# Gate and up biases of the routed experts: from one-hot matmul products to rows repeated by DMA and added by VectorE

## The reference

```
logits = xf @ router_w + router_b             # 32 experts, top 4 per token
gu  = xb @ w_gu[e] + b_gu[e]                  # xb: 128 tokens of expert e; w_gu[e] is 1024 x 2048
glu = minimum(gu[:, :1024], 7)                # the gate half
lin = clip(gu[:, 1024:], -7, 7)               # the up half
act = glu * sigmoid(1.702 * glu) * (lin + 1)
y   = act @ w_dn[e] + b_dn[e]                 # w_dn[e] is 1024 x 1024
```

## Time and profile before

| | |
|---|---|
| median of 3 runs | 2343.35 us (2341.95 to 2346.4) |
| the profiled execution, its own time | 2342.93 us |
| its span | 2341.1 us |
| mean granted TensorE clock | 0.948 of full |
| the 34 units | from about 825 us to 2308 us of the span |

### The profile page before, as it was taken

One profiled execution on the slowest core, in us unless ns is written; L12 is line 12 of the kernel. 1 busy time (PEld: TensorE's weight loads), 2 busy tenths in 40 slices (PEclk: granted clock), 3 DMA queues, 4 the chain that ended last, 5 costly groups with the idle time before them and its releaser, 6 DMA issues.

```text
span 2341.1 us, 41559 instructions
## 1 busy us (share of the span) xinstructions
PE 2165.4 (92%) x15487; PEld 1731.2 (74%) x15487; DVE 1834.0 (78%) x2152; ACT 1366.4 (58%) x1545; POOL 552.2 (24%) x434
## 2 busy tenths in 40 slices
PE   6899999867899399999999999999999999999994
PEld 5667888755678377778778778778778778778773
DVE  3699999948733777877877877877877877877885
ACT  4542223865742457667667667667667667667665
POOL 1007786764000102112112112112112112112110
PEclk8779999967999699999999999999999999999997
DMA  5011211020023279889889889889889889889896
GB/s 142 19 46 37 55 45 54 24 75 35 1 84 126 96 267 340 310 290 346 309 287 348 309 285 348 312 285 351 310 282 349 310 285 348 312 286 344 315 374 256
DMA packets 253598, 526.46 MB, mean 225 GB/s; under 512 B 33048, under 2 KB 59800, under 8 KB 253180
## 3 DMA queue, kind: packets, MB, share of 16 engines
q1 hardware_dynamic: 240268, 483.27, 57.6%
q0 software_dynamic: 13264, 42.34, 7.5%
HBM read 490.96 MB, written 35.91 MB: 225 GB/s over the span
## 4 chain that ended last, share of the span: by engine, by line
PE 70%; DMA 10%; DVE 8%; ACT 4%; issue 4%; POOL 2%; SPq 0%; DVEq 0%; ACTq 0%; POOLq 0%
PE ps L1754 13%; PE ps L1756 12%; PE ps L1755 12%; DMA e_raw<-in_w_gate_up_dram 9%; PE ps L1761 9%; PE ps L1429 5%; PE ps L1430 5%; PE ps L1431 5%; DVE e_wlo L2253 2%; PE ps L1766 1%; PE ps L1504 1%; PE ps L1634 1%; PE ps L1645 1%; PE ps L1584 1%; DVE a_s L2031 1%
## 5 line engine op out<-in xcount | busy, mean ns | idle before, releaser
L1312 ACT ACTIVATE e_whi<-e_raw 128x2048 fp32r<-128x2048 f32 x411 | 786.2, 1918 | 421.3 <-PE ps L1756 309.0
L2253 DVE TENSOR_TENSOR e_wlo<-e_raw,e_whi 128x2048 fp32r<-128x2048 f32 x410 | 926.8, 2286 | 66.3 <-ACT e_whi L1312 64.8
L1754 PE MATMUL ps<-e_whi,xh 128*128 128x512 f32 x1088 | 434.7, 400 | 0.0
L1755 PE MATMUL ps<-e_whi,xl 128*128 128x512 f32 x1088 | 424.3, 390 | 0.0
L1756 PE MATMUL ps<-e_wlo,xh 128*128 128x512 f32 x1088 | 424.1, 390 | 0.0
L941 POOL DMA_INDIRECT x_d<-ym,scur x34 | 70.6, 2078 | 871.0 <-ACT ym L1345 850.8
L1754 PEld LDWEIGHTS ps<-e_whi,xh 128*128 128x128 f32 x1088 | 204.3, 188 | 52.7 <-issue 12.9
L1756 PEld LDWEIGHTS ps<-e_wlo,xh 128*128 128x128 f32 x1088 | 204.3, 188 | 43.9
L1755 PEld LDWEIGHTS ps<-e_whi,xl 128*128 128x128 f32 x1088 | 204.5, 188 | 39.4
L1754 PE MATMUL ps<-e_whi,ath 128*128 128x512 f32 x544 | 221.7, 408 | 12.9 <-DVE atl L2281 12.9
L1756 PE MATMUL ps<-e_wlo,ath 128*128 128x512 f32 x544 | 213.3, 392 | 0.0
(11 more groups left out here) (351 smaller groups left out, 3345.1 us busy)
## 6 DMA issues: line engine op xcount, KB each, us to landing
e_raw<-in_w_gate_up_dram SPq DMA_DIRECT2D x275, 1024.0 KB, 5.2
e_raw<-in_w_down_dram SPq DMA_DIRECT2D x136, 1024.0 KB, 11.4
w_raw<-in_w_in_dram SPq DMA_DIRECT2D x20, 512.0 KB, 3.8
xt<-in_x_dram SPq DMA_DIRECT2D x8, 512.0 KB, 6.2
xr<-in_x_dram SPq DMA_DIRECT2D x8, 512.0 KB, 4.2
x_d<-x SPq DMA_DIRECT2D x8, 512.0 KB, 2.6
h_d<-h SPq DMA_DIRECT2D x8, 512.0 KB, 2.9
x<-x_d SPq DMA_DIRECT2D x8, 512.0 KB, 7.4
```

Of the source, the lines that this page charges most:

```text
L1312: nc.scalar.activation(e_whi[:, m % HRING, :], e_raw[:, m % RING, :], ACT.Copy).then_inc(s.e_hi, 1)
L1754: nc.tensor.matmul(dst, a_hi, slot_hi, start=False, stop=False, skip_group_check=True)
L1755: nc.tensor.matmul(dst, a_lo, slot_hi, start=False, stop=False, skip_group_check=True)
L2253: nc.vector.tensor_tensor(e_wlo[:, m % HRING, :], e_raw[:, m % RING, :], e_whi[:, m % HRING, :].bitcast(F32), ALU.subtract).then_inc(s.e_l ...
```

## The change

Gate and up biases no longer go through TensorE for the main tokens of a unit. SP loads the two bias rows of the unit's expert, each repeated into all 128 partitions, into `bgate` and `bup` (2 DMAs of 512 KB); VectorE adds them in place of the plain read of PSUM and limits the sum in a second operation, in place. The first product of a tile now starts the accumulation. SP issues the two loads for the next unit between its pieces 1 and 2, after a wait for the first operation of `a_out(1)` of the current unit, which is the last reader of the tiles. For the first unit they stand ahead of the store and the load of lines 733 and 734. The down bias and the biases of the overflow tokens stay as they were.

```diff
+        bgate = at("bgate", F_ + 108 * KB, [P, D])
+        bup = at("bup", F_ + 135 * KB, [P, D])
...
+            def load_biases(e):
+                for k, dst in enumerate((bgate, bup)):
+                    sp.dma_start(dst[:], I["b_gate_up"][0, bass.ds(e, 1), D * k:D * k + D].to_broadcast([P, D])).then_inc(s.ld_bgu, 16)
             def loads(u, here, after, following):
                 for m in range(3, PIECES):
                     load(u, m, here)
-                for m in range(3):
+                for m in range(2):
                     load(Unit(u.loop, u.a, u.b + 1, after), m, following)
+                sp.wait_ge(s.e_act, u.nth(12, 12 + 6 + 3))
+                load_biases(following)
+                load(Unit(u.loop, u.a, u.b + 1, after), 2, following)
...
             sp.wait_ge(s.v_be, BE_STEPS)
+            load_biases(e0)
...
             def sigmoid(u, j):
-                act.wait_ge(s.e_act, u.nth(8, 8 + 4 * j + 1))
+                act.wait_ge(s.e_act, u.nth(12, 12 + 6 * j + 2))
...
                 if half == 0:
-                    pe.wait_ge(s.e_act, u.nth(8, 4 * j + (6 if g else 5)))
-                    bias_into(ps[:, g, :], sel[:], D * g + 512 * j)
+                    pe.wait_ge(s.e_act, u.nth(12, 6 * j + (9 if g else 7)))
...
-                    m = three(ps[:, g, :], xh[:, buf, k, :], xl[:, buf, k, :], hi_[:, c, :], lo_[:, c, :], half == 1 and c == 3)
+                    m = three(ps[:, g, :], xh[:, buf, k, :], xl[:, buf, k, :], hi_[:, c, :], lo_[:, c, :], half == 1 and c == 3,
+                              k == 0)
...
             def g_out(u, j):
                 dve.wait_ge(s.p_pc, u.nth(PIECES, 4 * j + 2 + RING))
-                nc.vector.tensor_scalar(gm[:], ps[:, 0, :], LIMIT, None, ALU.min).then_inc(s.e_act, 1)
+                if j == 0:
+                    dve.wait_ge(s.ld_bgu, u.nth(32, 32))
+                nc.vector.tensor_tensor(gm[:], ps[:, 0, :], bgate[:, 512 * j:512 * j + 512], ALU.add).then_inc(s.e_act, 1)
+                dve.wait_ge(s.e_act, u.nth(12, 12 + 6 * j + 1))
+                nc.vector.tensor_scalar(gm[:], gm[:], LIMIT, None, ALU.min).then_inc(s.e_act, 1)
             def a_out(u, j):
                 dve.wait_ge(s.p_pc, u.nth(PIECES, 4 * j + 4 + RING))
-                nc.vector.tensor_scalar(um[:], ps[:, 1, :], LIMIT, -LIMIT, ALU.min, ALU.max).then_inc(s.e_act, 1)
-                dve.wait_ge(s.e_act, u.nth(8, 8 + 4 * j + 2))
+                nc.vector.tensor_tensor(um[:], ps[:, 1, :], bup[:, 512 * j:512 * j + 512], ALU.add).then_inc(s.e_act, 1)
+                dve.wait_ge(s.e_act, u.nth(12, 12 + 6 * j + 3))
+                nc.vector.tensor_scalar(um[:], um[:], LIMIT, -LIMIT, ALU.min, ALU.max).then_inc(s.e_act, 1)
+                dve.wait_ge(s.e_act, u.nth(12, 12 + 6 * j + 4))
```

More of the change, by code:

```diff
@@ L303, in __init__ @@
         self.ld_bias = sem("ld_bias")
+        self.ld_bgu = sem("ld_bgu")
         self.a_bias = sem("a_bias")
@@ L1750, in xo_transposes, with three @@
                 m.then_inc(s.p_xo, 1)
-            def three(dst, a_hi, a_lo, slot_hi, slot_lo, last):
-                nc.tensor.matmul(dst, a_hi, slot_hi, start=False, stop=False, skip_group_check=True)
+            def three(dst, a_hi, a_lo, slot_hi, slot_lo, last, first=False):
+                nc.tensor.matmul(dst, a_hi, slot_hi, start=first, stop=False, skip_group_check=True)
                 nc.tensor.matmul(dst, a_lo, slot_hi, start=False, stop=False, skip_group_check=True)
@@ L1798, in gu_step @@
                     k = 4 * half + c
-                    m = three(ps[:, g, :], xh[:, buf, k, :], xl[:, buf, k, :], hi_[:, c, :], lo_[:, c, :], half == 1 and c == 3)
+                    m = three(ps[:, g, :], xh[:, buf, k, :], xl[:, buf, k, :], hi_[:, c, :], lo_[:, c, :], half == 1 and c == 3,
+                              k == 0)
                 m.then_inc(s.p_pc, 1)
             def a_transposes(u, v, j):
-                pe.wait_ge(s.e_act, u.nth(8, 8 + 4 * j + 4))
+                pe.wait_ge(s.e_act, u.nth(12, 12 + 6 * j + 6))
                 for q in range(4):
@@ L2265, in g_out @@
                 dve.wait_ge(s.p_pc, u.nth(PIECES, 4 * j + 2 + RING))
-                nc.vector.tensor_scalar(gm[:], ps[:, 0, :], LIMIT, None, ALU.min).then_inc(s.e_act, 1)
+                if j == 0:
[3 more added lines that the diff above has]
+                nc.vector.tensor_scalar(gm[:], gm[:], LIMIT, None, ALU.min).then_inc(s.e_act, 1)
             def a_out(u, j):
                 dve.wait_ge(s.p_pc, u.nth(PIECES, 4 * j + 4 + RING))
-                nc.vector.tensor_scalar(um[:], ps[:, 1, :], LIMIT, -LIMIT, ALU.min, ALU.max).then_inc(s.e_act, 1)
-                dve.wait_ge(s.e_act, u.nth(8, 8 + 4 * j + 2))
+                nc.vector.tensor_tensor(um[:], ps[:, 1, :], bup[:, 512 * j:512 * j + 512], ALU.add).then_inc(s.e_act, 1)
+                dve.wait_ge(s.e_act, u.nth(12, 12 + 6 * j + 3))
+                nc.vector.tensor_scalar(um[:], um[:], LIMIT, -LIMIT, ALU.min, ALU.max).then_inc(s.e_act, 1)
+                dve.wait_ge(s.e_act, u.nth(12, 12 + 6 * j + 4))
                 nc.vector.scalar_tensor_tensor(out=um[:], in0=um[:], scalar=1.0, in1=gm[:], op0=ALU.add, op1=ALU.mult).then_inc(s.e_act, 1)
-                dve.wait_ge(s.e_act, u.nth(8, 8 + 4 * j + 3))
+                dve.wait_ge(s.e_act, u.nth(12, 12 + 6 * j + 5))
                 dve.wait_ge(s.e_sg, u.nth(2, j + 1))
@@ L2307, in _ @@
             nl = dve.value_load(nbi[0:1, 0:1], min_val=1, max_val=NLMAX)
-            dve.sem_inc(s.e_act, 8)
+            dve.sem_inc(s.e_act, 12)
             dve.sem_inc(s.e_over, 8)
-            dve.wait_ge(s.e_act, 8)
+            dve.wait_ge(s.e_act, 12)
             dve.wait_ge(s.e_over, 8)
```

## The result

The changed kernel takes 2373.63 us (2370.76 to 2381.47, 4 runs) against 2344.81 us (2341.95 to 2346.4, 4 runs): a ratio of 1.013, interval 1.0102 to 1.0157. The forecast was 2336.3, with 2320 to 2362 as its range: the change is slower, and by more than any case that was priced. Its profiled execution took 2372.47 us for a span of 2370.7.

A forecast was written before the change was run, and what follows sets the result against it. TensorE was taken to bound L, with VectorE and the DMA engines right behind it in S. Sixteen pairs at -0.91 + 0.1 (-13.0), start +3 and X +3 summed to -7.0 us: 2336.3 us, range 2320 to 2362.

The forecast's parts named there:

- So the delay is just hidden: L unit: piece 3 issued 4.8 us late, last piece landing about 1365, ScalarE's split of piece 5 only 0.4 us late.
- a margin of 0.5: L unit: VectorE's chain to `am` ends at 1378.8, TensorE's transposes begin at 1379.3, so it fits by about 0.5 us.
- rival 2: L unit: pieces 3 to 5 over 0.5 us later than worked out make `am` late for TensorE; 2360 us, chance 15%.
- Products: TensorE, every unit: four 128x512 products removed, saving 0.91 us a unit, 1.81 us a pair.
- VectorE's growth: VectorE, every unit: `g_out` grows by 0.55 us and `a_out` by 0.54, 2.2 us a unit, 4.4 a pair.
- S gives nothing: S unit: its 0.91 us go into waits at pieces 9 and 10, and it gets 0.1 us longer.
- rival 1: S unit: `atl` doesn't bind, so pairs give the whole 1.81 us; 2320 us, chance 12%.
- Start: First unit: biases ahead of the table's store cost +3 us, bounds 1 (issue alone) and 4.
- X units: X units with full DMA engines: bias loads delay pieces, +1.9 us in the first, +1 in the second, together +3.
- Rival 3: S unit: GpSimd slows the limit in `a_out(0)`, VectorE loses 1.8 us, pairs +0.5; 2357 us, chance 7%.
- Rival 4: S unit: close waits of 0.7 and 0.95 us lower TensorE's clock, each pair losing 1.6 us; 2362 us, chance 8%.
- Rival 5: A wash: limit at 0.69 us and L giving up part of its 0.91; 2341 to 2348 us, chance 18%.

The follow-up runs named there:

- The small scatter: Changed kernel with GpSimd's scatter of each S unit cut to 16 of its 128 rows; 2347.19 us, ratio 1.0004 to the kernel before.
- the two sets: Changed kernel with separate bias tiles for L and S, no current-unit wait there, `wn3` loaded after the loops; 2346.52 us, ratio 1.0004 to the kernel before.
- the kept wait: Changed kernel with SP's wait and both loads kept, each per-unit load cut from 1024 columns to 4; 2383.85 us, ratio 1.0164 to the kernel before.

## Why the prediction was wrong

**The step that failed** is in the DMAs: piece 3 "lands at 1359.7 (5.2 us), pieces 4 and 5 2.7 us apart behind it, the last at about 1365", and from it "So the delay is just hidden". Its first half held: SP's wait puts piece 3 back by 4.9 us (4.8 forecast), and everything behind it on the queue with it, the reads of the table too. What was mis-sized is the landing of the last piece. I took 2.7 us a piece from the full rate, in a stretch in which the data of GpSimd's scatter now falls. Before, pieces 3 to 5 had landed by 5.5 us behind the last product of S, and the scatter's data came after them; late by 4.9 us, piece 5 shares the engines with it. Six us of the changed kernel in which most of that data moves:

```profile
1374.00:1380.00 6.00, 5.84 (x88) 4.67 (x88) 4.02 (x5) 3.71 (x2) 0.00 (x0) 1.00 1.04 289
```

The engines are full (share 1.04) and move 289 GB/s, where the full stretch in the earlier trace rows had 368. The last piece comes at 13.0 in place of 10.3 us, 2.7 late against a margin of 0.5, and L takes 51.24 in place of 49.09. The small scatter, the two sets and the kept wait show each part.

The packets show how the two share the engines. SP's queue (q1) and GpSimd's (q0) from 1377.65 to 1379.65, packets, MB and share of 16 engines:

```profile
q0 software_dynamic: 80, 0.33, 81.8%
q1 hardware_dynamic: 80, 0.16, 24.5%
```

Packet by packet they are even, but a packet of the scatter (4 KB) holds its engine for 0.33 us and one of the weights (2 KB) for 0.10, so the weights are left with a quarter of the engines' time. The scatter is as slow by itself: in the kernel before, from 1361.78 to 1362.78, it had the engines alone.

```profile
q0 software_dynamic: 51, 0.21, 105.1%
```

The Trainium skill, DMA: Bandwidth & Descriptors, section "Queues, rings and completion order", says that each DMA engine takes turns between its queues at packet granularity. The 80 packets against 80 of the trace agree, if what the profile counts as a packet is what that section means; no run shows that.

That was rival 2. Its condition was put rightly ("once they come over 0.5 us later"); its chance was put too low, because the scatter was in no line of the working, though GpSimd's issue of it stood 2.5 us behind the last product of S in the trace of before as well. By its own rule, 2.7 us late changes a pair by -0.81 + 2.2 = +1.4, +22 for 16 pairs, and with the +6 for start and X units the time would be about 2371, close to the 2373.6 measured. What it named as its sign was one step off: TensorE waits in piece 5, for its low part, and not at the transposes behind it.

By the terms of the sum, for the profiled execution:

| term | forecast | measured |
|---|---|---|
| L | -0.91 each, -14.6 | +1.23 each, +18.4 in 15 |
| S | +0.1 each, +1.6 | +0.2 in 16 |
| start | +3 | +4.2, with the first L |
| X | +3 | +7.5 |
| ahead of the units | 0 | +0.4 |
| all | -7.0 | +30.7 to the end of the experts, +29.6 in the span |

- **Products.** 0.91 us a unit is right: L is 0.93 shorter wherever its pieces come in time (49.09 in seven kernels), S 0.94 once nothing holds it.
- **VectorE's growth** was sized somewhat too high: adds 0.682, limits 0.427 us, so 0.47 per pair of operations in place of 0.55. The growth fits in L in all of these kernels.
- **S gives nothing** was right, and for its main reason: the order of VectorE decides, and the wait at piece 10 grew to 0.94. It was right for a second reason too, which the working only saw at its first link: without any growth S is no shorter (37.64 in the median), since `ath` sits behind a split that waits for a DMA. So rival 1 was not there to be had by this change.
- **Start.** The biases ahead of the store put piece 3 of the first unit out at 832.44, 4.3 us later than the 828.10 of before (3.9 later if both are counted from the end of the stages ahead). I had 3, from issue and bytes, with 4 as the bound. The first unit is 4.2 longer, and that is the low end: in the seven experiments that keep these loads ahead of the store it took 83.3 to 85.5 us, 5 to 7 more than before. What the rest is was not followed up.
- **X units.** Forecast +1.9 and +1; measured +2.5 and +5.0. With neither wait nor loads they get shorter (38.57, 36.67), with the wait alone 42.81 and 40.23, and with both, but the scatter of S small, 39.37 and 41.81. So the first loses by its late pieces meeting the scatter of the last S, as L does. The second follows an X, whose scatter was never made small; that loads and waits each carry part there is likely (41.91 with both, 40.23 with the wait alone) and wasn't taken apart. I had priced bytes alone, and rested "+1" on DMA time that stands free in the average of the unit.
- **Rival 3** (GpSimd and the limit): not seen. The limits took 426 to 429 ns on one line and 426 to 477 on the other. 16 of the 136 overlapped an operation of GpSimd; 15 of these took 0.43 us as all others did, and one took the 477 ns. By the Trainium skill (SBUF — State Buffer, section "SBUF: two separate sides") whichever of the two starts first keeps the shared ports and the other blocks. In this kernel that is hardly tested: in 14 of the 16 the limit had begun first, and of the two in which GpSimd had, one limit took 0.43 us and the other is the one of 477 ns.
- **Rival 4** (the clock): not seen. It is 1.00 in S and L with waits of 0.94 and 1.30 us in them, and 0.96 in the first X unit, as in the earlier trace rows.
- **Rival 5**: the limit was shorter, not longer.

Still open: why SP stands 0.4 us longer in front of piece 3 when the bytes are gone, what makes the first unit of most experiments longer than that of the changed kernel, and how the loss in the second X unit divides.

## What to carry to other kernels

A small load put on a queue behind a new wait can cost far more by what stands behind it on that queue than by its bytes: find each later issue, put it back by the wait, and then ask which other transfers it now runs beside, since its landing time from the trace of before no longer holds. Where one resource is full and a wait stands at a single place, take the saving away step by step in that chain before you count it; here S was held by two things at once, and moving one operation of ScalarE ahead of a split that waits for a DMA gave more (0.54%) than the bias change did without it. A change that pays in one kind of unit and not in another can be made in that kind alone.

## What the runs showed of the hardware

- The limit on a 128x512 tile in SBUF with both constants in the instruction took 427 ns. The row of 505 ns takes its number from a column in SBUF, and I had taken them for the same form; no run changes that alone.
- A row repeated into all partitions costs about what as many ordinary bytes cost: the two 512 KB loads landed in 5.5 and 6.3 us in the median, beside 7.1 us for a 1 MB piece in the same kernel. Over the units SP's queue moved 34.6 MB more than without the loads (448.68 against 414.07) and held the 16 engines for 85 us more, 2.5 us a MB, beside 2.7 for the rest. With 2 KB of bytes left such a load still took 4.2 us (DMA issues of the run with the wait kept: KB each, median us from issue to landing):

```profile
bgate<-in_b_gate_up_dram SPq DMA_DIRECT2D x29, 2.0 KB, 4.2
```

- While a scatter with add from GpSimd was on its way, the DMA engines showed a full share at 289 GB/s over 6 us, against 361 to 370 over whole S units. Alone, it filled them (share 1.05) at 209 GB/s; beside the weights it sent packet for packet with them, and each of its 4 KB packets took over three times as long as a 2 KB one of the weights.
- SP's reads of the expert table between rounds lie between piece 2 and piece 3 of L: from 1358.85 to 1367.51 SP issued nothing. They are hidden until something in front of them is late.
